# Stick-breaking attention over a paged cache: two neighbouring keys on a partition, later keys summed by pairs

## The reference

```python
past_k = pool_k[page_table].reshape(Bd, P, H_C, HEAD_DIM)
...
z = jnp.einsum('bthe,bshe->bhts', q, k) * scale + b_sb[None, :, None, None]
log_stay = jnp.where(mask, jax.nn.log_sigmoid(-z), 0.0)
later = lax.cumsum(log_stay, axis=3, reverse=True) - log_stay
a = jnp.where(mask, jnp.exp(jax.nn.log_sigmoid(z) + later), 0.0)
return jnp.einsum('bhts,bshe->bthe', a, v)
```

## Time and profile before

| | before |
|---|---|
| median of 3 runs | 3723.75 us |
| the profiled execution | 3721.61 us |
| its span, first to last instruction | 3720.0 us |
| PE busy over the span | 3405.9 us (92%) |
| DVE busy | 2045.5 us (55%) |
| ACT busy | 1557.1 us (42%) |
| POOL busy | 706.7 us (19%) |
| read from HBM | 436.28 MB |

### The profile page before, as it was taken

How to read it: one execution, slowest core, us unless ns; L and a number is a source line. 1 busy time by engine, 2 the same in 40 slices (tenths; PEclk the granted TensorE clock), 3 DMA queues, 4 the chain that set the end, 5 groups by cost and what they waited for, 6 DMA issues and landing times. The chain is left out here.

```text
span 3720.0 us, 61127 instructions
## 1 busy us (share of the span) xinstructions
PE 3405.9 (92%) x21973; PEld 2930.7 (79%) x21973; DVE 2045.5 (55%) x4143; ACT 1557.1 (42%) x3047; POOL 706.7 (19%) x986
## 2 busy tenths in 40 slices
PE   8999999989995999589997968999989999899996
PEld 7999999944443666356665858999989999899996
DVE  2211134468995665436664446656675665756664
ACT  3321122268882444224442225444454443544342
POOL 0111111156771334114440011000010000100000
PEclk9999999989996989789998988999999999999998
DMA  5654456421005541669984552434353444422222
GB/s 202 216 193 164 149 177 194 151 66 43 10 10 117 107 87 41 234 235 331 354 302 145 174 184 93 132 118 155 127 166 122 139 135 142 149 85 77 72 69 77
DMA packets 435826, 533.92 MB, mean 144 GB/s; under 512 B 93749, under 2 KB 370870, under 8 KB 430550
## 3 DMA queue, kind: packets, MB, share of 16 engines
q1 hardware_dynamic: 407214, 416.41, 36.1%
q10 hardware_dynamic: 11946, 63.40, 5.0%
q0 software_dynamic: 16384, 50.35, 3.8%
HBM read 436.28 MB, written 143.91 MB: 156 GB/s over the span
## 5 line engine op out<-in xcount | busy, mean ns | idle before, releaser
L3519 PE MATMUL p_DP<-p_UH,p_WH 128*128 128x352 f32 x1536 | 497.7, 324 | 20.7 <-issue 14.4
L3520 PE MATMUL p_DP<-p_UL,p_WH 128*128 128x352 f32 x1536 | 496.7, 323 | 0.0
L3521 PE MATMUL p_DP<-p_UH,p_WL 128*128 128x352 f32 x1536 | 496.6, 323 | 0.0
L3519 PE MATMUL p_UP<-p_TH,p_WH 128*128 128x352 f32 x1344 | 439.4, 327 | 53.0 <-DVE p_TL L3429 36.9
L3520 PE MATMUL p_UP<-p_TL,p_WH 128*128 128x352 f32 x1344 | 434.1, 323 | 0.0
L3521 PE MATMUL p_UP<-p_TH,p_WL 128*128 128x352 f32 x1344 | 434.0, 323 | 0.0
L916 PE MATMUL p_PP<-p_WH,p_HH 128*128 128x384 f32 (+1 forms) x1224 | 420.1, 343 | 9.2 <-DVE p_WL L618 4.8
L917 PE MATMUL p_PP<-p_WL,p_HH 128*128 128x384 f32 (+1 forms) x1224 | 408.5, 334 | 0.0
L918 PE MATMUL p_PP<-p_WH,p_HL 128*128 128x384 f32 (+1 forms) x1224 | 407.9, 333 | 0.0
L603 ACT ACTIVATE p_PT<-p_PP,p_rs 128x384 f32<-128x384 f32 (+1 forms) x153 | 87.3, 570 | 539.3 <-PE p_PP L918 539.3
L3519 PEld LDWEIGHTS p_DP<-p_UH,p_WH 128*128 128x128 f32 x1536 | 290.9, 189 | 23.0 <-issue 21.8
(11 more groups left out here) (445 smaller groups left out, 6677.9 us busy)
## 6 DMA issues: line engine op xcount, KB each, us to landing
p_WU<-in_w_up SPq DMA_DIRECT2D x48, 1024.0 KB, 5.4
p_WD<-in_w_down SPq DMA_DIRECT2D x192, 256.0 KB, 2.9
cw_K<-in_cache_sb_k SPq DMA_DIRECT2D x192, 192.0 KB, 4.3
cw_V<-in_cache_sb_v POOLq DMA_DIRECT2D x192, 192.0 KB, 5.1
out_s_wk<-in_cache_win_k ACTq DMA_DIRECT2D x64, 382.5 KB, 3.5
out_s_wv<-in_cache_win_v ACTq DMA_DIRECT2D x64, 382.5 KB, 4.2
p_HH<-scratch_xh SPq DMA_DIRECT2D x34, 512.0 KB, 4.8
p_HL<-scratch_xl SPq DMA_DIRECT2D x34, 512.0 KB, 5.5
```

Of the source, the lines that this page charges most:

```text
L3519: pe.matmul(out, hi, rhi, start=first, stop=False, skip_group_check=True)
L3520: pe.matmul(out, hi, rlo, start=False, stop=False, skip_group_check=True)
L3521: return pe.matmul(out, lo, rhi, start=False, stop=last, skip_group_check=True)
```

## The change

A page now lies on 64 partitions. Key pair p of the page (keys 2p and 2p + 1, neighbours in memory, 3072 bytes) goes to one partition; page i of the group goes to partitions 64 to 127 where i is even and 0 to 63 where it is odd, into slots 2(i // 2) and 2(i // 2) + 1. There are still 8 DMAs of 192 KB for a group, each now of 64 rows of 3072 bytes.

The later keys follow this order. DVE adds the two keys of a partition, DS = L[even] + L[odd] (192 columns), runs four running sums over DS in place of eight over L, and takes each key's own terms off its logit in ZB (L[odd] from the odd slots, DS from the even ones, 192 columns each). PE multiplies a strict triangle with DS and ones with SL, 192 columns each, and `exponents` adds the result to both keys of a pair by a broadcast. `keys(n + 1, 5)` stands behind all of this. POOL makes one more constant matrix, `nlate`, at the start of the phase.

```diff
     def load(self, eng, dst, src, landed, pages, q):
-        for r in range(self.NP):
-            eng.dma_start(dst[q][:, r, :], src[bass.ds(pages[self.NP - 1 - r], 1), :, :].rearrange("a p c -> p (a c)")).then_inc(landed[q], 16)
+        for i in range(self.NP):
+            page = src[bass.ds(pages[self.NP - 1 - i], 1), :, :].rearrange("a (p e) c -> (a p) (e c)", e=2)
+            half, r = (1 - i % 2) * P // 2, i // 2
+            eng.dma_start(dst[q][half:half + P // 2, 2 * r:2 * r + 2, :].rearrange("p e c -> p (e c)"), page).then_inc(landed[q], 16)
...
+            pool.affine_select(out=nlate[:, :], in_=nlate[:, :], compare_op=ALU.is_gt, fill=0.0, base=0,
+                               pattern=[[-1, P]], channel_multiplier=1).then_inc(consts, 1)
...
-                ins = dve.tensor_tensor(AR[:, :, :], ZB[n % 2][:, :, :], AP_[:, :, :], ALU.add)
+                dve.wait_ge(own_ok, 2 * n + 2)
+                ins = dve.tensor_tensor(AR[:, :, :].rearrange("p (r e) c -> p r e c", e=2), ZB[n % 2][:, :, :].rearrange("p (r e) c -> p r e c", e=2),
+                                        LATER[:, :, None, :].broadcast_to([P, NR, 2, C]), ALU.add)
...
-                for r in range(NP):
-                    dve.wait_ge(s_ok, n * (NP + 1) + r + 1)
-                    dve.tensor_tensor(SL[s][:, r + 1, :], SL[s][:, r, :], L[s][:, r, :], ALU.add).then_inc(s_ok, 1)
-                    if n + 1 < N and r == 4:
-                        keys(n + 1, 5)
-                dve.wait_ge(s_ok, n * (NP + 1) + NP + 1)
+                dve.tensor_tensor(DS[s][:, :, :], L[s][:, 0:NP:2, :], L[s][:, 1:NP:2, :], ALU.add).then_inc(two_ok, 1)
+                dve.tensor_tensor(ZB[s][:, 1:NP:2, :], ZB[s][:, 1:NP:2, :], L[s][:, 1:NP:2, :], ALU.subtract).then_inc(own_ok, 1)
+                dve.wait_ge(two_ok, n + 1)
+                for r in range(NR):
+                    dve.wait_ge(s_ok, n * (NR + 1) + r + 1)
+                    dve.tensor_tensor(SL[s][:, r + 1, :], SL[s][:, r, :], DS[s][:, r, :], ALU.add).then_inc(s_ok, 1)
+                dve.tensor_tensor(ZB[s][:, 0:NP:2, :], ZB[s][:, 0:NP:2, :], DS[s][:, :, :], ALU.subtract).then_inc(own_ok, 1)
+                if n + 1 < N:
+                    keys(n + 1, 5)
+                dve.wait_ge(s_ok, (n + 1) * (NR + 1))
...
-                pe.matmul(AP_[:, :, :], ntri[:, :], L[n % 2][:, :, :], start=True, stop=False)
-                pe.matmul(AP_[:, :, :], nones[:, :], SL[n % 2][:, 0:NP, :], start=False, stop=True).then_inc(arg_ok, 1)
+                pe.matmul(LATER, nlate[:, :], DS[n % 2][:, :, :], start=True, stop=False)
+                pe.matmul(LATER, nones[:, :], SL[n % 2][:, 0:NR, :], start=False, stop=True).then_inc(arg_ok, 1)
```

More of the change, by code:

```diff
@@ L2373, in stick_sample_phase @@
     BANKS = 3
+    NR = NP // 2
     FROM_ACT = (0, 2, 4)
@@ L2390, in stick_sample_phase @@
         L = [m.sb(f"L{i}", [P, NP, C]) for i in range(2)]
-        SL = [m.sb(f"SL{i}", [P, NP + 1, C]) for i in range(2)]
+        DS = [m.sb(f"DS{i}", [P, NR, C]) for i in range(2)]
+        SL = [m.sb(f"SL{i}", [P, NR + 1, C]) for i in range(2)]
         AR = m.sb("AR", [P, NP, C])
@@ L2403, in stick_sample_phase @@
         ntri = m.sb("ntri", [P, P])
+        nlate = m.sb("nlate", [P, P])
         nones = m.sb("nones", [P, P])
@@ L2431, in stick_sample_phase @@
         arg_ok = m.sem("arg_ok")
+        two_ok, own_ok = m.sem("two_ok"), m.sem("own_ok")
         ar_ok = m.sem("ar_ok")
@@ L2450, in stick_sample_phase @@
         AP_ = APB[:, 0:NP * C].rearrange("p (r c) -> p r c", c=C)
+        LATER = APB[:, 0:NR * C].rearrange("p (r c) -> p r c", c=C)
         FIN = APB[:, NP * C:NP * C + C].rearrange("p (g c) -> p g c", g=PAIRS)
@@ L2461, in _ @@
             pool.memset(maskn[:, :, :], 0.0)
-            for t in (ntri, nones):
+            for t in (ntri, nlate, nones):
                 ins = pool.memset(t[:, :], -1.0)
@@ L2469, in _ @@
                                pattern=[[-1, P]], channel_multiplier=1).then_inc(consts, 1)
-            pool.wait_ge(consts, 3)
+            pool.affine_select(out=nlate[:, :], in_=nlate[:, :], compare_op=ALU.is_gt, fill=0.0, base=0,
+                               pattern=[[-1, P]], channel_multiplier=1).then_inc(consts, 1)
+            pool.wait_ge(consts, 4)
             new = maskn[:, :, :].rearrange("p b (h t) -> p b h t", h=2)
@@ L2474, in _ @@
                                pattern=[[-DT, DB], [0, 2], [0, DT]], channel_multiplier=1).then_inc(consts, 1)
-            pool.wait_ge(consts, 4)
+            pool.wait_ge(consts, 5)
             pool.affine_select(out=new, in_=new, compare_op=ALU.is_gt, fill=NEG, base=0,
@@ L2479, in _ @@
             for c in range(P // HW):
-                pool.wait_ge(consts, 5 + c)
+                pool.wait_ge(consts, 6 + c)
                 pool.affine_select(out=fold[:, :], in_=fold[:, :], compare_op=ALU.not_equal, fill=1.0, base=-c * HW,
@@ L2617, in _ @@
             dve.wait_ge(zn_ok, 1)
-            dve.wait_ge(consts, 5)
+            dve.wait_ge(consts, 6)
             for g in range(PAIRS):
@@ L2644, in _ @@
                     exponents(n - 1)
-                src = SI[:, b, :] if q == 0 else SL[1 - s][:, NP, :]
+                src = SI[:, b, :] if q == 0 else SL[1 - s][:, NR, :]
                 dve.tensor_copy(SL[s][:, 0, :], src).then_inc(s_ok, 1)
@@ L2676, in new_sums @@
             def new_sums():
-                pe.wait_ge(consts, 9)
+                pe.wait_ge(consts, 10)
                 pe.wait_ge(si_ok, 1)
@@ L2728, in cumulate @@
             def cumulate(n):
-                pe.wait_ge(s_ok, (n + 1) * (NP + 1))
+                pe.wait_ge(s_ok, (n + 1) * (NR + 1))
                 pe.wait_ge(yn_ok, 1)
```

## The result

The change makes the kernel slower: median 3817.78 us (3800.3 to 3827.95, 4 runs) against 3724.15 us (3720.0 to 3727.45, 4 runs), ratio 1.0249 with a 95% interval of 1.0222 to 1.0276. That is +93.6 us by the medians. The profiled execution of the changed kernel took 3827.95 us with a span of 3826.3, 106.3 above the span of before; it is the slowest of its four runs.

The account below looks back on a forecast made before the run. PE with its chain paces the phase, the DMA engines barely keeping up; 64-partition loads at 228 GB/s then add 107 us, hiding the -5.3 us saved. 3721.6 + 107 = 3828.7, or 3830.8 against the median, said as 3830; range 3717 to 3878.

Parts of the forecast that it names:

- Rate: Loads inside the phase: 91.2 MB on 64 partitions at 228 GB/s take 400 us, making the phase 107 us longer.
- the bounds (205 to 282): Load rate in GB/s: 205 would cost +152 us; 282, with queues on opposite halves half the time, +30.
- The tail: End of the phase: 8.0 us from the last values to the next phase's first load, so it ends at 2082.5.
- The start: Phase's loads issued from about 1674.5 us; the 48 DMAs before the phase need 41 of 67 us: 0.
- The products: PE's `cumulate`: 0.66 us less, but T waits for the logarithm, so an ordinary group saves 0; wait 0.42 to 1.08.
- Groups with the fold: Seven groups where T waits for AR and the fold's totals: 0.66 us less each, 4.6 us saved.
- The sum without the loss: Whole kernel if loads keep up: only -5.3 us from folds and phase end, +0.1 for the start, is left.
- The moved copy: DVE's `keys(n + 1, 5)` starts 2.68 us after L, still before the second half of `logits` reads it: 0.
- the four sums: DVE's running sums, four replacing eight: 0.94 us less, ending 0.2 us earlier after L than the eight.
- The partial one: Loads in the phase: halves collide only in part, 282 to 303 GB/s, +30 to +8 us, 3731 to 3754; chance 0.11.
- The one without loss: Loads in the phase: two queues reach the needed 355 GB/s, only -5.3 + 0.1 us is left, 3718.6; chance 0.17.
- The faster one: Ordinary groups: if T could start with AR, 31 x 0.66 = 20.5 us come through, 3703; chance 0.05.

Follow-up runs that it names:

- first run: The changed kernel with the loads of the kernel before (128 partitions, 1536-byte rows), computation of the change kept: 3705.99 us, ratio 0.9969.
- second: The kernel before with only the loads of the change (64 partitions, 3072-byte rows): 3815.97 us, ratio 1.0257.
- third: The changed kernel with a page on every second partition instead of on one half, triangle reordered to match: 3710.75 us, ratio 0.9979.
- fourth: The changed kernel with 64-partition loads for the keys only, values loaded as before: 3771.51 us, ratio 1.0147.
- fifth: The changed kernel with GpSimd issuing the value pages of each pair in the other order, odd page first: 3820.98 us, ratio 1.0269.

## Why the prediction was right, and where its sum was not

**The cause and the sign** held. 64-partition loads, read off, are the whole loss: it goes with them (first run), comes with them (second), and goes with the choice of partitions alone (third).

**The size** came out close partly because two terms missed in opposite directions. Forecast +107 us for the profiled execution, +106.3 measured there, which is luck to this degree; by the medians the change is +93.6, and its runs spread over 28 us where those of before spread over 7.

- Rate: taken as 228 GB/s, measured 246 to 248 with two queues. The loads took from 1679.5 to about 2052 us, 372.5 instead of 400: 27.5 us too much in the forecast. That two queues of other rows gain some 8% over the one of the earlier trace rows had no row; the bounds (205 to 282) held it.
- The tail: taken as 8.0 us from the end of the loads to the next phase, on the tacit assumption that the last values land last and nothing but their products is left. The DMA share is down to 0.01 from 2052 us on, and the next phase starts at 2082.87. What came in last were keys as well: group 30's arrived at 2043.5, and three groups still had to pass through PE.

```profile
2043.51 1.97 PE L2720 MATMUL sc_KTP<-sc_ident,cw_K 128*128 128x128 f32 x8 [8.56 <-DMA cw_K<-in_cache_sb_k]
...
2053.68 1.06 PE L2730 MATMUL sc_ZT<-sc_KT,sc_QD 128*32 128x512 f32 x6
...
2062.67 1.06 PE L2730 MATMUL sc_ZT<-sc_KT,sc_QD 128*32 128x512 f32 x6
...
2074.86 1.52 PE L2763 MATMUL sc_YP<-sc_VP,sc_T 128*32 128x128 f32 x48 [1.35 <-ACT sc_T L2535]
```

  From the end of the loads it is 30.9 us and not 8.0: the pipeline's depth, some 23 us, was left out.
- The start: the phase's first load went out at 1679.5 us, not at 1674.6. The forecast had 0 for the loads before the phase. But three runs with the same early key loads (the second, fourth and fifth) reached the first product at 1672.32, 1669.73 and 1672.89, earlier than before's 1677.38 and the change's 1681.86. So these 5 us are not a cost of the loads; where they arise between executions is not known.

The three misses, +5, -27.5 and +23 us, leave 0.4 us: the phase was forecast to end at 2082.5 and ended at 2082.87.

**The products** in ordinary groups: 0.64 us less work, as forecast (0.66), and the wait grew as forecast in kind, but to 0.86 us, not 1.08. Saved were 0.15 us per group where I had 0. The step that failed is that T's two conditions met within 0.01 us, so I took either for the limit. With AR out of the way T starts 0.09 us before the logarithm has ended, where before it started 0.04 after it. In the changed kernel itself this is hidden by the loads; it shows in the first run.

**Groups with the fold**: forecast -0.66 each, measured 9.63 to 9.00, -0.63.

**The sum without the loss.** In the first run the part from the first product to the next phase's first load is 292.2 us against 298.3, -6.1, where -5.3 + 0.1 was forecast: close, but by other terms. From the third group to the last it is 250.5 us against 258.2, -7.7: seven folds, and 22 ordinary groups that were priced at 0. The first two groups take 1.2 us more and the end 0.3 more, where -0.7 was forecast. In both places PE's granted clock is lower than before (0.84 against 0.92 in the first two groups, 0.87 against 1.00 in the last). The median of that run is 13 us lower, which the phase explains by half; the rest lies outside it or in the spread, and stays open.

**The moved copy**: forecast 2.68 us after L. In the first run L starts at 1858.03 and the copy at 1860.29, 2.26 us: the 192-column operations last 0.36 us, as taken from the bias row, but start 0.27 apart, since consecutive ones that don't depend on each other overlap. In such a group the second half of `logits` (1861.88) did not wait for it. In the last group, where PE has no keys left to turn in between, it did, by 1.0 us, in the changed kernel and in the first run alike:

```profile
2064.76 1.06 PE L2730 MATMUL sc_ZT<-sc_KT,sc_QD 128*32 128x512 f32 x6 [1.02 <-DVE sc_KT L2586]
```

In the kernel before, PE waits 0.78 us at this place, for ACT. The prediction had 0 for the copy. It also has the four sums end 0.2 us earlier after L than the eight: this left out the copy that stood between the eight, and it is 0.9 us (2.98 to 2.08).

**The rivals.** The partial one would have needed a rate above 282 GB/s. The one without loss would be right for a page on every second partition. The faster one named the right lever, T's place: with T, the sums of the later keys and bank 5 moved, an undisturbed group is 0.96 us shorter, though not from the change as it stands.

The rule cited from the Trainium skill, "SBUF — State Buffer", section "Door 1: The DMA port swizzle", is that 64 neighbouring partitions reach 8 of 16 ports, some 218 GB/s at most; that two DMAs on the two halves gain 6% stands in the same page's section "Can I just issue two DMAs to hit both halves?". The runs agree with the loss, and with a small gain from a second queue, but both rates lie above the page's: 228 GB/s for one queue and 246 for two, where 218 and, as an estimate by its 6%, 231 were to be expected. The section on Door 1 maps partitions to ports by bits 2 to 4 and 6 of their number. By that map every second partition reaches all 16 ports, and the 365 GB/s agree; the ports themselves are not in the trace.

## What to carry to other kernels

Before a load is narrowed to fewer partitions, look in the trace for a stretch whose DMA share is full and compare its GB/s with that of full-width loads: the share alone does not tell a slow path from a used one. Where half the partitions must do, try every second one and reorder the small constant matrices: here that gave back all of the rate. And when work is cut on an engine, look first for what the next stage waits for: here an in-order queue kept most of the saving (0.49 of 0.64 us in an ordinary group) until the waiting steps themselves were moved.

## What the runs showed that was not expected

**PE's clock is lower behind a wait for loads.** So such a group takes longer than by its wait alone. After, the granted clock is 0.88 from 1700 to 1900 us where it was 1.00 before; right after the first wait (stretches as above):

```profile
1727.00:1737.00 10.00, 8.23 (x118) 6.15 (x121) 7.61 (x21) 5.59 (x11) 4.18 (x8) 1.00 1.02 240
1737.00:1741.50 4.50, 1.80 (x42) 0.89 (x33) 1.79 (x7) 0.59 (x1) 2.49 (x5) 1.00 1.04 242
1741.60:1745.00 3.40, 3.40 (x15) 1.41 (x15) 0.69 (x1) 0.60 (x1) 1.55 (x3) 0.56 1.03 239
```

PE idled for 2.77 us, and in the stretch behind it the clock is 0.56, mostly the lower of its two levels (1.2 GHz). Six products of 512 columns take 1.93 us there, not 1.06. From the third group to the last the changed kernel takes 359.0 us and the first run 250.5. Of the 108.5 us between them 80.9 are waits for key loads; the waits ahead of the values hardly differ (28.0 and 26.3 us). Most of the other 27 us is thus PE at work at the lower clock. Since the loads pace the phase this is hidden in its middle, but PE is then slower just when keys have arrived.

**A long landing time is not a slow queue.** Landing takes 26.6 us for keys and 11.6 for values, with rows of the same length in both, and PE's load waits are all for keys. Yet the two queues move nearly the same from 1700 to 1900 us (packets, MB, share of the 16 engines; q0 carries the values, q1 the keys):

```profile
q0 software_dynamic: 6144, 25.17, 53.0%
q1 hardware_dynamic: 9701, 23.85, 49.6%
...
POOL cw_V L2082 <- PE sc_YP L2763: 170.8, 21, 17.8
```

What differs is how much is asked for at once. An estimate from these rows: 26.6 us at 23.85 MB in 200 us is 3.2 MB in flight, 16 loads or two groups of keys; 11.6 us at 25.17 MB is 1.5 MB, seven loads or about one group of values. SP shows no wait for PE from 1700 to 2050 us, where the kernel before had 27.9 us of such waits to 1950: it always has the next keys to ask for. GpSimd stood waiting for PE to use a group's values instead (the last row, 1690 to 2080 us, one of two tiles), so its queue held little. Why it is the keys and not the values that fall behind was not tested.
